# Key norms by logarithm and exponential, and a new order of work, in the first stage of a second block

## The reference, cut to what matters

```python
p = x @ w_in
fox_cols = p[..., :FOX_COLS]
rwkv_cols = _token_shift(p[..., FOX_COLS:FOX_COLS + RWKV_COLS], rwkv_mu)   # p + mu * (prev - p)
...
decay = jnp.exp(-jnp.exp(-jax.nn.softplus(-w_pre) - 0.5))
a = jax.nn.sigmoid((a0 + a_lora @ a2).astype(f32))
kk = heads(k * k_k)
kk = kk / jnp.maximum(jnp.sqrt(jnp.sum(kk * kk, axis=-1, keepdims=True)), 1e-12)
k_mod = k.astype(f32) * (1.0 + (a - 1.0) * k_a.astype(f32))
...
log_f = jax.nn.log_sigmoid(f_logit.astype(jnp.float32))      # forget gate of the attention, 8 heads
```

## Time and profile before

| | |
|---|---|
| median of three timed runs | 1415.6 us (1414.64 to 1416.53) |
| the profiled execution's own time | 1418.0 us |
| its span, first to last instruction | 1416.3 us |
| mean granted clock of TensorE | 0.994 |
| TensorE busy | 1382.9 us, 98% |
| VectorE busy | 892.2 us, 63% |
| ScalarE busy | 869.3 us, 61% |
| GpSimd busy | 764.5 us, 54% |
| share of the chain of waits | TensorE 70%, GpSimd 12%, VectorE 6%, ScalarE 2% |

### The profile page before, as it was taken

The page is one execution under the profiler, slowest core; times in us unless marked ns, Lnnn a source line. Parts: engine busy times, 40 slices in busy tenths (PEclk is TensorE's granted clock), DMA queues, the critical chain, the costliest instruction groups (busy, mean ns, idle before and its releaser), DMA issues.

```text
span 1416.3 us, 28596 instructions
## 1 busy us (share of the span) xinstructions
PE 1382.9 (98%) x9422; PEld 1220.7 (86%) x9422; DVE 892.2 (63%) x1967; ACT 869.3 (61%) x1496; POOL 764.5 (54%) x350
## 2 busy tenths in 40 slices
PE   7999999999999999999999999999999999999997
PEld 6878888887888777789999999999998888888886
DVE  3784883214753654435998049999977776655555
ACT  5475775446755656556666768888874544444443
POOL 6876889877765523877988877777750000000000
PEclk9999999999999999999999999999999999999999
DMA  6633566555443312654555556566559877666662
GB/s 199 209 124 119 193 194 194 185 185 166 147 149 122 127 53 75 208 187 155 193 178 188 180 175 201 190 201 198 200 189 329 273 243 240 208 193 191 194 193 96
DMA packets 75352, 256.63 MB, mean 181 GB/s; under 512 B 8472, under 2 KB 8856, under 8 KB 75032
## 3 DMA queue, kind: packets, MB, share of 16 engines
q1 hardware_dynamic: 64192, 231.76, 50.2%
q10 hardware_dynamic: 11096, 24.00, 4.9%
HBM read 244.72 MB, written 11.01 MB: 181 GB/s over the span
## 4 chain that ended last, share of the span: by engine, by line
PE 70%; POOL 12%; issue 8%; DVE 6%; ACT 2%; DMA 0%; POOLq 0%; ACTq 0%; DVEq 0%
PE PS L1079 60%; POOL WL L403 12%; PE PS L1124 2%; PE PS L1637 2%; PE PS L1458 1%; PE PS L1125 1%; PE PS L1416 0%; DVE GA L1804 0%; DMA fbias<-fox_bias 0%; PE PS L1363 0%; DVE H L1994 0%; DVE XS L2270 0%; DVE GA L1803 0%; DVE BK L2008 0%; PE PS L1613 0%
## 5 line engine op out<-in xcount | busy, mean ns | idle before, releaser
L403 POOL TENSOR_TENSOR WL<-RAW,WH 128x1024 fp32r<-128x1024 f32 x306 | 740.2, 2429 | 278.6 <-ACT WH L462 190.8
L1079 PE MATMUL PS<-XHL,WH 128*128 128x256 f32 x2528 | 460.8, 284 | 2.2 <-DVE XHL L1757 1.5
L953 ACT CAST WH<-RAW 128x1024 fp32r<-128x1024 f32 x252 | 263.6, 1046 | 226.5 <-PE PS L1079 211.6
L1079 PEld LDWEIGHTS PS<-XHL,WH 128*128 128x128 f32 x2528 | 394.5, 192 | 5.8 <-issue 4.0
L1079 PE MATMUL PS<-XHL,WL 128*128 128x256 f32 x1264 | 357.8, 283 | 0.0
L462 ACT CAST WH<-RAW 128x1024 fp32r<-128x1024 f32 x184 | 191.3, 1047 | 109.4 <-PE PS L1079 98.7
L1079 PEld LDWEIGHTS PS<-XHL,WL 128*128 128x128 f32 x1264 | 242.7, 192 | 0.0
L2440 DVE TENSOR_TENSOR WL<-RAW,WH 128x1024 fp32r<-128x1024 f32 x128 | 156.8, 1225 | 120.2 <-ACT WH L953 119.5
L1079 PE MATMUL PS<-WH,CH 128*128 128x512 f32 x512 | 199.2, 389 | 0.0
L1079 PE MATMUL PS<-WH,CL 128*128 128x512 f32 x512 | 199.2, 389 | 0.0
L1079 PE MATMUL PS<-WL,CH 128*128 128x512 f32 x512 | 199.2, 389 | 0.0
(11 more groups left out here) (407 smaller groups left out, 1966.4 us busy)
## 6 DMA issues: line engine op xcount, KB each, us to landing
RAW<-weights SPq DMA_DIRECT2D x438, 512.0 KB, 3.6
gates_rest<-stage ACTq DMA_DIRECT2D x32, 272.0 KB, 2.2
stage<-gates_rest ACTq DMA_DIRECT2D x32, 272.0 KB, 4.1
H<-x SPq DMA_DIRECT2D x2, 512.0 KB, 4.8
LG<-rows ACTq DMA_DIRECT2D x2, 512.0 KB, 6.3
LB<-rows ACTq DMA_DIRECT2D x2, 512.0 KB, 8.8
x<-H ACTq DMA_DIRECT2D x1, 1024.0 KB, 5.8
HY<-x ACTq DMA_DIRECT2D x1, 1024.0 KB, 13.4
```

Source lines behind the costliest of these rows:

```text
L403: nc.gpsimd.tensor_tensor(WL[:, slot, :], RAW[:, slot, :], plain(WH[:, slot, :]), ALU.subtract).then_inc(w_lo, 1)
L953: nc.scalar.copy(WH[:, slot, :], RAW[:, slot, :]).then_inc(w_hi, 1)
L1079: last = mm(dst, a, b, start=start and k == 0, stop=stop and k == len(pairs) - 1)
```

## The change

On ScalarE, the cast ahead of a chunk's mu product moves behind it from chunk 8 on, and for chunk 7 it moves behind the whole key-norm branch. The k_a factor goes to banks 0 and 1 in PSUM (UU is gone), once the sum over time has been read. The root and VectorE's reciprocal become ScalarE's logarithm in place and exponential with a factor -0.5. The value copies start a chunk sooner. On VectorE, the first key directions come before shift(9), and chunk 13 is rescaled and shifted before the second CR product. On TensorE, the transposes no longer wait for BK and CR, only the scores do; the forget gate's product goes to bank 6 and waits for the seventh scaled chunk of fox_qk there, and the wait for the last token-major copy moves to the first gate item.

```diff
             def times_mu(m):
-                feed(FIRST["rwkv"] + m)
+                if m < 7:
+                    feed(FIRST["rwkv"] + m)
...
                 A(Z[:, m % 4, 1:S + 1], PS[:, second_bank(m), 0:S], ACT.Copy, scale=col("mu", m)).then_inc(sem("z_ready"), 1)
+                if m >= 8:
+                    feed(FIRST["rwkv"] + m)
...
                 if m == 7:
                     act.wait_ge(sem("sig_ready"), 2)
+                    act.wait_ge(sem("cum_ready"), 1)
                     for c in range(4):
-                        last = A(UU[:, c, :], four(2)[:, c, :], ACT.Identity, scale=col("k_a", c),
+                        last = A(four(0)[:, c, :], four(2)[:, c, :], ACT.Identity, scale=col("k_a", c),
                                  bias=ST[:, 100 + c:101 + c])
                     last.then_inc(sem("scaled_ready"), 1)
-                    root(PS[0:RH, 7, 0:S], PS[0:RH, 7, 0:S], 8)
+                    act.wait_ge(sem("ms_ready"), 8)
+                    A(PS[0:RH, 7, 0:S], PS[0:RH, 7, 0:S], ACT.Ln).then_inc(sem("sq_ready"), 1)
+                    act.wait_ge(sem("sq_ready"), 8)
+                    A(rn8[:, :], PS[0:RH, 7, 0:S], ACT.Exp, scale=-0.5).then_inc(sem("rn_ready"), 1)
+                    feed(FIRST["rwkv"] + 7)
                 if m == 9:
-                    act.wait_ge(sem("cum_ready"), 1)
+                    act.wait_ge(sem("keys_ready"), 1)
                     A(four(0), cum[:, :, :], ACT.Exp, scale=DECAY).then_inc(sem("growth_ready"), 1)
...
-                if m >= 12:
-                    value_rows(m - 12)
-            for q in range(2, NPAIR):
-                value_rows(q)
+                if m >= 11:
+                    value_rows(m - 11)
+            value_rows(NPAIR - 1)
...
                     wait("nk_ready", 2)
-                    wait("bk_ready", 1)
                 if m:
                     by_token(m - 1)
+                if m == 1:
+                    wait("bk_ready", 1)
                 if m % 2:
                     r_scores(m // 2)
...
             by_token(7)
-            wait("tok_ready", 2 * NCH)
-            small_gates(PS[0:FH, 7, 0:S], FWH, FWL).then_inc(sem("f_mm"), 1)
+            wait("fqk_out", 7)
+            small_gates(PS[0:FH, 6, 0:S], FWH, FWL).then_inc(sem("f_mm"), 1)
...
+                if j == 0:
+                    wait("tok_ready", 2 * NCH)
...
             rescale(8)
-            wait("sq_ready", 8)
-            V.reciprocal(rn8[:, :], PS[0:RH, 7, 0:S]).then_inc(sem("rn_ready"), 1)
             shift(8)
             wait("scaled_ready", 1)
-            V.tensor_tensor(KM[:, :, :], UU[:, :, :], SH[:, K_AT:K_AT + 4, :], ALU.mult).then_inc(sem("keys_ready"), 1)
+            V.tensor_tensor(KM[:, :, :], four(0), SH[:, K_AT:K_AT + 4, :], ALU.mult).then_inc(sem("keys_ready"), 1)
             rescale(9)
+            key_directions(0)
             shift(9)
-            key_directions(0)
...
+            rescale(13)
+            shift(13)
             wait("sh_ready", R_AT + 4)
             V.tensor_tensor(part(CR, 1), chunked(SH[:, R_AT:R_AT + 4, :]), chunked(decays), ALU.mult).then_inc(
                 sem("bk_ready"), 1)
-            rescale(13)
-            shift(13)
...
-            link(V.tensor_tensor(fr[:, 0, :], PS[0:FH, 7, 0:S], RB[0:FH, :], ALU.mult))
+            link(V.tensor_tensor(fr[:, 0, :], PS[0:FH, 6, 0:S], RB[0:FH, :], ALU.mult))
```

More of the change, by code:

```diff
@@ L212, in bass_blocks @@
         cum = at("cum", [P, 4, S], F32, A0 + 20480)
-        UU = at("UU", [P, 4, S], F32, A0 + 28672)
         NKK = at("NKK", [P, 4, S], F32, A0 + 57344)
```

## The result

The changed kernel took 1417.83 us, median of 12 runs (1416.56 to 1420.0), against 1416.18 us, median of 12 runs of the kernel before beside it: ratio 1.0015, interval 1.0008 to 1.0022. The forecast was 1414.3, a little faster. The measured time is 1.65 us above the kernel before beside it: a difference of less than 0.2%, but with an interval wholly above 1, and 1417.83 lies above the range's end of 1417.0.

The account below looks back on a forecast made before the run. TensorE, busy 98% of the span, was taken to bound the kernel. Values +0.29, clock at the transposes -1.88, forget gate -1.15 and clock at item 10 +1.4 gave -1.3 us: 1414.3 from 1415.6, range 1411.4 to 1417.0.

Parts of the forecast that it names:

- item 10's weights late, at full clock: Tenth weight tile, cast behind the key norms: TensorE waits until 382.7, so rescale(10) starts later, +0.35 us.
- low clock in item 10: Tenth weight tile's product: likely partly at half clock after 3.8 us with only 1.0 of key norms, +1.4 us.
- cast ahead of the second exponential: ScalarE: item 15's cast now stands between chunk 12's mu product and the second growth exponential, +0.95 us.
- one-column copy: VectorE's copy of one NKK column into CR: no step of its own, covered by unchanged full-length steps, 0.
- chunk 13 ahead of the CR product: VectorE: rescale(13) and shift(13) come earlier, ahead of the second CR product, -1.13 us.
- forget gate: Forget gate's product no longer waits for the copy out of bank 7, -1.15 us.
- Clock at the transposes: Value transposes: the long idle stretch splits into 0.9 and 0.3, so the clock stays full, -1.88 us.
- From rescale(10) to the values: VectorE and ScalarE up to the values: +0.35 carried on, casts and moves added, sum +0.29 us.
- a rival, at 0.12 and +0.5: Clock fall at 402 is no habit, so no 1.88 to gain: +0.5 us, 1416.1, chance 0.12.
- no second table load: Key norms on ScalarE: logarithm and exponential share a table, branch 1.28 earlier: -4.0 us, 1411.6, chance 0.04.
- the clock holds: Rival at item 10, the tenth weight tile: no low clock there, -2.7 us, 1412.9, chance 0.20.
- The low clock lasts: Rival from item 10 on: half clock continues, item 10 loses 2.9 us; with all six items +3.1, 1418.7; chance 0.04.

Follow-up runs that it names:

- warm: Changed kernel with 18 products nobody reads put into TensorE's wait ahead of item 10 (tenth weight tile): 1416.45 us, ratio 1.0001 to the kernel before.
- after_again: The changed kernel, unchanged, timed and profiled once more: 1418.08 us, ratio 1.0018 to the kernel before.
- fgate: The kernel before with only the forget gate's product moved to bank 6: 1415.17 us, ratio 0.9994 to the kernel before.
- before_again: The kernel before, unchanged, timed and profiled once more: 1415.8 us, ratio 0.9999.
- copy_early: Changed kernel with the one-column copy of NKK into CR moved ahead of VectorE's wait for the second growth exponential: 1416.9 us, ratio 1.0005 to the kernel before.
- casts_in_front: Changed kernel with every cast back ahead of its chunk's mu product, one-column copy left in place: 1410.7 us, ratio 0.9961 to the kernel before.
- norms_first: Changed kernel with casts ahead of mu products, one-column copy early, and logarithm and exponential ahead of the k_a products: 1413.31 us, ratio 0.9980 to the kernel before.
- early7: Changed kernel with the cast of item 10's weights put back ahead of chunk 7's mu product: 1414.29 us, ratio 0.9992 to the kernel before.
- values_alone: The kernel before with only the values mixed sooner (value copies, chunk 13's rescale and shift, scores alone waiting): 1413.93 us, ratio 0.9983 to the kernel before.
- ln_alone: The kernel before with only root and reciprocal replaced by ScalarE's logarithm and exponential, factor in SBUF: 1416.15 us, ratio 1.0008 to the kernel before.

## Why the prediction was wrong

Most of its chain came as written. Two terms failed, a gain that was mostly never there and a delay that was put at nothing, and they turned a small gain into a small loss. By terms, from the profiles:

| step | predicted | measured |
|---|---|---|
| item 10's weights late, at full clock | +0.35 | +0.76 (rescale(10) of warm less that of before) |
| low clock in item 10 | +1.4 | +1.46; +2.3 in after_again (38.78 less 36.49) |
| cast ahead of the second exponential | +0.95 | +0.94 |
| one-column copy | 0 | +1.28 |
| chunk 13 ahead of the CR product | -1.13 | -1.13 |
| cast among the value copies | +0.12 | +0.10 |
| full clock at the transposes | -1.88 | -1.47, where the clock had fallen |
| forget gate | -1.15 | -1.41 |
| stage | -1.3 | +0.53 |

The rows "cast ahead" and "chunk 13" are from the distances between rescale(12), the exponential and rescale(13); the last two from fgate, before_again and before.

**The first failed step is "Clock at the transposes", "I take the whole 1.88 as gained".** The low clock there was in one of three profiles of the kernel's old order at this place (before, and not fgate, which idled as long in front of them, nor before_again). As far as three profiles tell, the median holds only a part of it, so most of this term was never there to gain. I had this as a rival, at 0.12 and +0.5. Its size too was misread: behind the wait the transposes take 0.66 at full clock and not 0.44, and an item behind the scores 3.07 and not 2.88 (404.29 and 406.03 in the chain above); the price is 0.45 + 0.92 + 0.10 = 1.47, which is also 84.81 - 83.34.

**The second is in "From rescale(10) to the values": "each step is at full length".** I carried VectorE's instructions over with their lengths, and moved GpSimd's subtractions in time without asking which of them would now meet. The late cast of item 15 put a subtraction over the copy: +1.28 (copy_early, casts_in_front). The Trainium skill's page "SBUF — State Buffer", section "Who interferes with whom", says that a copy between two places of SBUF can hold, or be kept out by GpSimd from, a pair of ports that the two engines share, for a whole instruction; the trace agrees, 1.45 ended with GpSimd's 2.38.

The kernel before already had such a meeting, and the prediction misread it. Its key product, both operands in SBUF, ran from 379.62 to 382.10, begun while GpSimd subtracted (from 378.67), and GpSimd's next subtraction took 3.37 where the others take 2.4. VectorE's own subtractions of two SBUF operands of this size, late in the kernel with GpSimd idle, took 1.22:

```profile
380.98 3.37 POOL L403 TENSOR_TENSOR WL<-RAW,WH 128x1024 fp32r<-128x1024 f32 x1
1114.49 1.22 DVE L2440 TENSOR_TENSOR WL<-RAW,WH 128x1024 fp32r<-128x1024 f32 x1
```

So the 2.48 of the earlier trace rows was most likely half waiting, and not the length of a product of two SBUF operands. With the factor in PSUM it took 1.22 even beside a subtraction (379.71, GpSimd from 378.98). No run has this product in SBUF with GpSimd idle, so this much is argued.

**Smaller, item 10's weights:** +0.76 for +0.35. Item 10 begins 0.1 later than the 382.7 of the prediction (33.2 of the stage, 382.8 on the old scale), and takes 3.12 at full clock (warm) where the prediction took a later item's 2.88.

Put together against the old order without the fall (83.34): without the 1.88, with 1.28 for the copy and 0.41 for item 10, and with 0.26 more from the forget gate, the -1.3 becomes +2.0. The two profiles of the changed kernel are 2.0 and 2.8 us longer than 83.34, beside 1.65 and, in the second series, 2.5 (ratio 1.0018) of the whole. The first profile pair shows only 0.53, because the kernel before had its unlucky fall in it.

What held: the two table loads, and norms ready at 379.3 on the old scale (377.96 with the start 1.33 sooner); the wait of 2.4 for GpSimd at item 10 with half clock behind it; no low clock at the transposes; no wait at the forget gate. The rivals "no second table load" and "the clock holds" are refuted. "The low clock lasts" came in part, 7.0 us in after_again: it cost item 10 2.3 (5.46 for 3.12), where that rival had 2.9, and the rest of it fell into waiting.

Behind the stage, the changed kernel's profiles have 6.8 us of low clock from 504.6, where before it was 3.4, and take 0.9 to 1.7 us more there than the two of the kernel before. It isn't tied to the change alone: warm, fgate and norms_first show the long form too, the other kernels the short one. But both profiles of the changed kernel have it, and neither of the kernel before. How often each comes in the timed runs stays open, and with it 1 us or more of any single comparison, the 1.65 too.

## What to carry to other kernels

A producer's step moved behind a dependent chain "because there is time" must be followed through every engine that it feeds: here one cast of 1.03 held back GpSimd, a weight tile, and through the clock 1.5 us more. The whole change cost 0.15%; the same parts with the casts left in front of the waits gave 0.4 to 0.5%. When an instruction in a row takes twice what its like takes, look for what ran beside it before carrying its length over. And before a low clock is entered as a gain, see it in more than one execution.

## What the runs showed of the hardware

- The same idle 2.15 us of TensorE brought the clock to 0.50 in one execution (before) and left it at 1.00 in another (fgate). Behind two short waits of 0.55 and 0.81 with an item between, it fell in before_again and values_alone, and stayed at 1.00 in before and fgate. With 2.38 us idle behind small products, item 10 ran at low clock in each of the three profiles that had the gap unfilled (changed, after_again, copy_early), at a loss of 1.4 to 1.5 us, or 2.3 in after_again, where the fall came inside the wait.
- A VectorE copy of 16 elements per partition between SBUF addresses took 1.45 us for 0.17 when it met a running GpSimd subtraction, in all four profiles in which it did (changed, early7, warm, after_again). A copy of that size from PSUM took 0.17 beside the subtraction (copy_early).
- A VectorE product of 128x1024 with both operands in SBUF took 2.48 to 2.76 us beside GpSimd's subtractions (before, before_again, fgate, values_alone, ln_alone); with one operand in PSUM 1.22 beside them (changed).
- The logarithm, 8x256 in PSUM, took 0.34 and the exponential 0.37, as the root's 0.33.
